# Trunk kernel: the last down weights through the freed up-weight places, the end of the split and tap order, and the last two layer-norm tiles in halves

## The reference, cut to what matters

```python
def conv_glu_ffn(x, w_up, conv_w, conv_b, w_down):
    up = causal_depthwise_conv(x @ w_up, conv_w, conv_b)     # width 3 along the sequence
    gate, val = up[..., :D_FF], up[..., D_FF:]
    return (jax.nn.silu(gate) * val) @ w_down

ffn = conv_glu_ffn(x, ffn_w_up, ffn_conv_w, ffn_conv_b, ffn_w_down)
ple = jax.nn.sigmoid(x @ ple_w_gate) * (p @ ple_w_proj)
x = layer_norm(DEEPNORM_ALPHA * x + ffn + ple, ln2_g, ln2_b)
```

## Time and profile before

| what | before |
| --- | --- |
| median of 3 runs | 1392.42 us (1392.4 to 1392.64) |
| the profiled execution, its own time | 1391.88 us |
| its span | 1389.8 us |
| TensorE busy | 1311.3 us |
| VectorE busy | 860.7 us |
| ScalarE busy | 502.4 us |
| GpSimd busy | 233.2 us |
| mean granted TensorE clock | 0.983 |

### The profile page before, as it was taken

How to read it: one execution, slowest core, us unless ns; L and a number is a source line. 1 busy time by engine, 2 the same in 40 slices (tenths; PEclk the granted TensorE clock), 3 DMA queues, 4 the chain that set the end, 5 groups by cost and what they waited for, 6 DMA issues and landing times.

```text
span 1389.8 us, 16699 instructions
## 1 busy us (share of the span) xinstructions
PE 1311.3 (94%) x6276; PEld 1064.6 (77%) x6276; DVE 860.7 (62%) x1041; ACT 502.4 (36%) x744; POOL 233.2 (17%) x152
## 2 busy tenths in 40 slices
PE   6999999989956999899999999999999999999986
PEld 5787787767855788788888877878787787888785
DVE  3545646544298844633367767677676867677655
ACT  4435545545424322511332423323242323324411
POOL 0000000002182000430001121211111221111125
PEclk9999999989988999999999999999999999999998
DMA  5101101000000311210111201011111101011202
GB/s 224 46 31 31 42 19 45 32 23 24 1 0 32 121 61 62 91 46 31 46 46 46 76 31 60 31 60 45 45 60 59 61 30 60 30 61 46 76 31 106
DMA packets 22948, 71.95 MB, mean 52 GB/s; under 512 B 2544, under 2 KB 2800, under 8 KB 22896
## 3 DMA queue, kind: packets, MB, share of 16 engines
q1 hardware_dynamic: 22896, 71.22, 15.2%
HBM read 67.02 MB, written 4.19 MB: 51 GB/s over the span
## 4 chain that ended last, share of the span: by engine, by line
PE 68%; DVE 12%; ACT 4%; issue 3%; DMA 2%; DVEq 0%; SPq 0%; ACTq 0%
PE ps L677 12%; PE ps L679 12%; PE ps L678 12%; PE ps L1020 7%; PE ps L1018 7%; PE ps L1019 7%; PE ps L771 2%; DMA down_raw<-u_down 2%; DVE conv_ff L1804 1%; ACT conv_ff L1381 1%; PE ps L731 1%; PE ps L755 1%; PE ps L814 1%; DVE w_lo L563 1%; PE ps L1049 1%
## 5 line engine op out<-in xcount | busy, mean ns | idle before, releaser
L677 PE MATMUL ps<-x_hi,w_hi 128*128 128x512 f32 x336 | 141.7, 422 | 14.2 <-DVE x_lo L507 10.6
L678 PE MATMUL ps<-x_lo,w_hi 128*128 128x512 f32 x336 | 134.1, 399 | 0.0
L679 PE MATMUL ps<-x_hi,w_lo 128*128 128x512 f32 x336 | 133.9, 398 | 0.0
L1855 DVE TENSOR_TENSOR acc<-acc,ps 128x512 f32<-128x512 f32 x144 | 96.1, 685 | 53.4 <-PE ps L679 52.9
L1018 PE MATMUL ps<-mix_hi,w_hi 128*128 128x512 f32 x320 | 126.6, 396 | 0.0
L1019 PE MATMUL ps<-mix_lo,w_hi 128*128 128x512 f32 x320 | 126.6, 396 | 0.0
L1020 PE MATMUL ps<-mix_hi,w_lo 128*128 128x512 f32 x320 | 126.6, 396 | 0.0
L677 PE MATMUL ps<-h_hi,w_hi 128*128 128x512 f32 x288 | 114.6, 398 | 1.5 <-DVE acc L1855 1.5
L679 PE MATMUL ps<-h_hi,w_lo 128*128 128x512 f32 x288 | 113.9, 396 | 0.0
L678 PE MATMUL ps<-h_lo,w_hi 128*128 128x512 f32 x288 | 113.9, 395 | 0.0
L2105 POOL TENSOR_TENSOR weight_sums<-raw 128x512 f32<-128x512 f32 x20 | 28.9, 1443 | 493.1 <-DMA raw<-u_up 493.1
(11 more groups left out here) (256 smaller groups left out, 2916.5 us busy)
## 6 DMA issues: line engine op xcount, KB each, us to landing
raw<-u_up SPq DMA_DIRECT2D x44, 512.0 KB, 3.3
raw<-u_in SPq DMA_DIRECT2D x22, 512.0 KB, 3.3
down_raw<-u_down SPq DMA_DIRECT2D x44, 256.0 KB, 2.8
x_stage<-u_x SPq DMA_DIRECT2D x8, 512.0 KB, 8.1
raw<-u_out SPq DMA_DIRECT2D x8, 512.0 KB, 3.2
x_nat<-x_nat SPq DMA_DIRECT2D x8, 512.0 KB, 3.3
raw<-u_gate SPq DMA_DIRECT2D x8, 512.0 KB, 3.3
out<-o_norm SPq DMA_DIRECT2D x8, 512.0 KB, 2.6
```

The lines of the kernel that those rows point to most:

```text
L677: mm(dst, w_hi, x_hi, start=first, stop=False)
L678: mm(dst, w_hi, x_lo, start=False, stop=False)
L679: return mm(dst, w_lo, x_hi, start=False, stop=last)
L1855: v.tensor_tensor(dst, dst, ps[:, DOWN_BANKS[k % 4], :], ALU.add).then_inc(dn_added, 1)
```

## The change

Six edits, all behind the last chunk's up products:

1. D0A/D0B and D1A/D1B of `pp` 1 come as two whole rows of 512 KB into `raw_a` and `raw_b`, each as soon as the last up operand in its place is split. Only D0B/D1B of `pp` 0 still goes through `down_raw`, and it stands ahead of `ln_gain` and `ln_bias` in SyncE's queue.
2. ScalarE and VectorE split the down operands in another order: D0A, D1A of `pp` 0 ahead of h's split, then D0B, D1B of `pp` 1, D0B, D1B of `pp` 0, then D0A and, last, D1A of `pp` 1. `TAIL_SLOT` keeps the places.
3. The taps of the last gate row are split around `combine` step 5, and ScalarE's second `tap` comes ahead of `silu`.
4. In quarter 0, k 2 waits for D0A of `pp` 1 alone, k 3 for D1A.
5. Tile 2q-1 is turned after `jp` 1 instead of `jp` 2, and `affine` follows the statistics at once, ahead of the next `add_last`. `statistics` waits per half.
6. Tiles 6 and 7 are turned in halves: the first half of tile 6 before `jp` 3 of the last quarter, then the first half of 7, the second of 6, the second of 7. Tile 6 is normalized on ScalarE; gain and bias of its first 512 columns are done on GpSimd, of its last 512 on VectorE behind tile 7, which VectorE still does whole. Tile 7 is stored first.

The diff, cut to its core:

```diff
 TAIL_OPS = ([(o, 0) for o in OPERANDS + (A22,)] + [(o, 1) for o in OPERANDS + (A22,)]
-            + [(d, k) for k in range(2) for d in (D0A, D1A, D0B, D1B)])
+            + [(D0A, 0), (D1A, 0), (D0B, 1), (D1B, 1), (D0B, 0), (D1B, 0), (D0A, 1), (D1A, 1)])
+TAIL_SLOT = {(D0A, 0): 0, (D1A, 0): 1, (D0B, 0): 2, (D1B, 0): 3, (D0A, 1): 4, (D1A, 1): 5}
...
+        for i, (o, r) in enumerate(((S4, raw_a), (A22, raw_b))):
+            eng.wait_ge(op_lo_done, lo_count(LASTC, o, 1))
+            eng.dma_start(raw[:, r, :], a["u_down"][2 * LASTC + i]).then_inc(raw_in[r], 16)
+        eng.wait_ge(op_lo_done, lo_count(LASTC, D1A, 0))
+        load_down(LASTC - 1, D0B)
         eng.wait_ge(prod_full, product_count(LASTC, S2, 1))
         eng.dma_start(lng[:, :], a["ln2_g"].partition_broadcast(P)).then_inc(ln_in, 16)
         eng.dma_start(lnb[:, :], a["ln2_b"].partition_broadcast(P)).then_inc(ln_in, 16)
-        eng.wait_ge(op_lo_done, lo_count(LASTC, D1A, 0))
-        load_down(LASTC - 1, D0B)
-        eng.wait_ge(op_lo_done, lo_count(LASTC, D1B, 0))
-        load_down(LASTC, D0A)
-        eng.wait_ge(op_lo_done, lo_count(LASTC, D1A, 1))
-        load_down(LASTC, D0B)
...
+            for h in halves:
+                eng.wait_ge(dn_added, 16 * (LASTC - 1) + 4 * (m // 2) + 2 * h + 2)
+                for kt in range(4 * h, 4 * h + 4):
+                    last = turn(two((1, 3)[m % 2])[:, kt * P:(kt + 1) * P], acc[:, kt, m * P:(m + 1) * P])
+                last.then_inc(o_full, 1)
...
-                if jp in (0, 2):
-                    turn_back(2 * q - 2 + jp // 2)
-        for m in range(MT - 2, MT):
-            turn_back(m)
+                if jp < 2:
+                    turn_back(2 * q - 2 + jp)
+                elif q == 3 and jp == 2:
+                    turn_back(MT - 2, (0,))
+        turn_back(MT - 1, (0,))
+        turn_back(MT - 2, (1,))
+        turn_back(MT - 1, (1,))
...
+        final_statistics(n, (0,))
+        final_statistics(m, (1,))
+        final_statistics(n, (1,))
+        affine(m)
+        eng.wait_ge(stored[n % 4], 16)
+        v.scalar_tensor_tensor(out=y, in0=rows(n), scalar=st[:, n, 12:13], in1=lng[:, :], op0=ALU.subtract,
+                               op1=ALU.mult).then_inc(o_cent, 1)
+        eng.wait_ge(o_sqrt, n + 1)
+        link(v.reciprocal(st[:, n, 13:14], st[:, n, 15:16]))
+        eng.wait_ge(o_cent, 1)
+        v.scalar_tensor_tensor(out=y, in0=y, scalar=st[:, n, 13:14], in1=lnb[:, :], op0=ALU.mult,
+                               op1=ALU.add).then_inc(o_last, 1)
+        eng.wait_ge(o_nrm, m + 1)
+        y = on[:, m % 4, HALF:D]
+        link(v.tensor_tensor(y, y, lng[:, HALF:D], ALU.mult))
+        v.tensor_tensor(y, y, lnb[:, HALF:D], ALU.add).then_inc(o_last, 1)
...
+        m = MT - 2
+        y = on[:, m % 4, 0:HALF]
+        eng.wait_ge(o_nrm, m + 1)
+        link(g.tensor_tensor(y, y, lng[:, 0:HALF], ALU.mult))
+        g.tensor_tensor(y, y, lnb[:, 0:HALF], ALU.add).then_inc(o_bias, 1)
```

More of the change, by code:

```diff
@@ L516, in op_place, with op_raw @@
             return (last_l if lo else last_h)[:, (D0B, D1B).index(o), :]
-        s_ = (position(c, o, pp) + 4) % 6
+        s_ = TAIL_SLOT[(o, pp)] if c == LASTC and o not in PRODUCTS else (position(c, o, pp) + 4) % 6
         return (wl if lo else wh)[:, s_ // 2, s_ % 2 * HALF:(s_ % 2 + 1) * HALF]
-    def op_raw(o):
+    def op_raw(c, o, pp):
+        if c == LASTC and pp and o not in PRODUCTS:
+            return raw[:, raw_a if o in (D0A, D0B) else raw_b, (slice(0, HALF) if o in (D0A, D1A) else slice(HALF, D))]
         return {A11: raw[:, raw_a, 0:HALF], A12: raw[:, raw_a, HALF:D], A22: raw[:, raw_b, HALF:D],
@@ L528, in wait_op_raw @@
         pair = 2 * (c - 1) + pp
-        if o in (A11, A12):
+        if c == LASTC and pp and o not in PRODUCTS:
+            r = raw_a if o in (D0A, D0B) else raw_b
+            eng.wait_ge(raw_in[r], 16 * (loads_before[r] + 2 * LASTC + 1))
+        elif o in (A11, A12):
             eng.wait_ge(raw_in[raw_a], 16 * (loads_before[raw_a] + pair + 1) + 32 * it)
@@ L1106, in chunk, with turn_back @@
             odd(c, it)
-        def turn_back(m):
-            if m % 2 == 0:
-                eng.wait_ge(dn_added, 16 * (LASTC - 1) + 4 * (m // 2 + 1))
+        def turn_back(m, halves=(0, 1)):
             if m == 0:
                 eng.wait_ge(row_done, 4 * CHUNKS)
-            elif m >= 2:
+            elif m >= 2 and 0 in halves:
                 eng.wait_ge(o_nrm, m - 1)
-            for kt in range(KT):
-                last = turn(two((1, 3)[m % 2])[:, kt * P:(kt + 1) * P], acc[:, kt, m * P:(m + 1) * P])
-            last.then_inc(o_full, 1)
+            for h in halves:
[3 more added lines that the diff above has]
+                last.then_inc(o_full, 1)
         for t in range(4):
@@ L1483, in _ @@
         op_hi(c, A22, 1)
-        h_high(c, 0)
         op_hi(c, D0A, 0)
         op_hi(c, D1A, 0)
-        tap(c, 1, 0)
+        h_high(c, 0)
+        op_hi(c, D0B, 1)
+        op_hi(c, D1B, 1)
         op_hi(c, D0B, 0)
         op_hi(c, D1B, 0)
+        tap(c, 1, 0)
+        op_hi(c, D0A, 1)
+        tap(c, 1, 1)
         silu(c, 1)
-        tap(c, 1, 1)
-        op_hi(c, D0A, 1)
         op_hi(c, D1A, 1)
-        op_hi(c, D0B, 1)
-        op_hi(c, D1B, 1)
         h_high(c, 1)
@@ L1961, in _ @@
         op_lo(c, A22, 1)
+        op_lo(c, D0A, 0)
+        op_lo(c, D1A, 0)
         h_low(c, 0)
-        op_lo(c, D0A, 0)
         combine(c, 1, 3)
-        op_lo(c, D1A, 0)
+        op_lo(c, D0B, 1)
+        op_lo(c, D1B, 1)
         combine(c, 1, 4)
-        taps(c, 1, 0)
         op_lo(c, D0B, 0)
         op_lo(c, D1B, 0)
+        taps(c, 1, 0, 0, (1,))
         combine(c, 1, 5)
+        taps(c, 1, 0, 0, (2,))
         op_lo(c, D0A, 1)
-        op_lo(c, D1A, 1)
         taps(c, 1, 1)
         glu(c, 1)
-        op_lo(c, D0B, 1)
-        op_lo(c, D1B, 1)
+        op_lo(c, D1A, 1)
         h_low(c, 1)
```

77 lines of the change are left out of this document (42 added, 35 removed).

## The result

| | before | changed |
| --- | --- | --- |
| median of 6 runs each | 1392.05 us | 1382.63 us (1380.5 to 1386.39) |
| ratio, changed to before | | 0.9937, interval 0.9921 to 0.9953 |
| span of the profiled execution | 1389.8 us | 1380.0 us |
| mean granted clock | 0.983 | 0.985 |

The change makes the kernel faster by 0.5 to 0.8%. The forecast of 1381.1 us was 1.5 us too low and inside the changed kernel's own runs; the range of 1378.0 to 1385.5 holds the median and five of the six runs. The forecast gave no spread for the runs: these six lie over 5.9 us, and eleven of the kernel before, timed beside `a2_changed`, over 5.5. Some of the experiments ask what part one pair of loads has in it.

A forecast was written before the change was run, and what follows sets the result against it. TensorE, busy 1311.3 of 1389.8 us, was taken as the bound, with losses in quarter 0 and a serial VectorE end. Terms -9.4 + 0.4 - 2.3 = -11.3 gave 1381.1 us, range 1378.0 to 1385.5.

The forecast's parts named there:

- The way in: Last 90 us: TensorE loses 11.0 us in quarter 0 to late weight splits and slow clock; VectorE's chain bounds the end.
- Term one: Quarter 0 of `last_down`: quarter 1 starts at 1325.3 instead of 1334.70, -9.4 us.
- the landing L: When the D0B/D1B pair of `pp` 0 lands, before quarter 0: forecast 1310.2, bounds 1309.3 and 1311.3.
- L to h: Serial ScalarE and VectorE work from the pair's landing to h's low part, feeding quarter 0's k 3: 12.2 us.
- The clock: Quarter 0: idle of 1.6 us, less than the 2.45 after which the clock stayed full, so no slow products.
- Term two: Quarters 1 to 3: half a turn of tile 6 newly on TensorE's path in front of `jp` 3, +0.4 us.
- Term three: The end, after the last `add_last`: five operations laid end to end finish at 10.15 instead of 12.4 us, -2.3 us.
- The sum: Whole kernel: -9.4 + 0.4 - 2.3 = -11.3 us, forecast median 1381.1 us.
- The late pair with a cold array: Quarter 0: late pair makes TensorE idle 3.6 us, clock drops, slow products cost 2.1 us; 1385.2 us, chance 0.15.
- The end gives nothing: The end: tile 6's half waits behind GpSimd's earlier tiles or a store, term three is lost; 1383.4 us, chance 0.1.
- they overlap after all: The end: the last VectorE and GpSimd operations run at once; 1379.1 us, chance 0.08.
- The slower case: Before quarter 0: `raw_b`'s row lands at 1320.5 or later and all 11.3 us are lost; past 1392.4 us, chance 0.03.

The follow-up runs named there:

- a2_changed: The changed kernel itself, run once more unaltered against the kernel before; 1382.12 us, ratio 0.9929.
- e3_ln_after: The changed kernel with one wait more: the two layer-norm loads are issued only after the pair for `down_raw` has landed; 1381.42 us, ratio 0.9919.
- e5_old_order: The changed kernel with whole-row loads kept, but splits, taps and TensorE's waits in the order of the kernel before; 1385.32 us, ratio 0.9957.
- e2_tail: The kernel before with only the changed turns, end order and handling of tiles 6 and 7; 1390.63 us, ratio 0.9987.
- e6_no_pool: The changed kernel with tile 6's gain and bias done whole on VectorE, none on GpSimd; 1382.70 us, ratio 0.9930.
- e1_head: The changed kernel with turns, end order and tiles 6 and 7 as in the kernel before; 1387.42 us, ratio 0.9966.
- e8_turns_back: The changed kernel with the odd tiles turned after `jp` 2 again, as in the kernel before; 1382.06 us, ratio 0.9930.
- e4_ln_ahead: The changed kernel with the two layer-norm loads issued ahead of the pair for `down_raw`; 1386.73 us, ratio 0.9956.

## Why the prediction was right, point by point

**The way in.** Two waits of 2.45 and 5.67 and a cold array in quarter 0, and a serial end: both were the places, and behind quarter 0's start nothing else moved by more than 0.5 us.

**Term one, -9.4: measured -8.7** in the profiled execution, -7.6 in a2_changed. What was off is mostly the landing L, the time of one pair of loads. I took 3.08 + 0.9 us from the second issue; it was 4.38 here and up to 6.82 elsewhere. That is 0.4 of the missing 0.7; another 0.2 is that the second of the pair was issued that much later, counted from quarter 0's start. The 0.9 came from one row, `ln_gain` with one load behind it. The pair has a row ahead and two behind, and e3_ln_after shows what it is without the two behind: 3.8. Against that the five traces with them are 0.4 to 3.0 longer. So my 3.98 had the right size for a pair with the row alone beside it, and for another reason than the one that I gave. Everything behind L held: L to h was forecast at 12.2 us and took 12.2 (1311.54 to 1323.73), and did so in every trace where this line bounds. The loads give 6.2 of the 8.7 and the order 2.5, by e5_old_order; I hadn't divided it.

**The clock.** That no product was slow came true, but the reason that I gave, an idle time shorter than the 2.45 that had left the clock full, is not enough. In e2_tail a wait of 2.31 us was followed by twelve products, and the clock fell while TensorE was still at them; the section on the hardware has the rows. In the traces with the changed kernel's order no clock fell where one wait stood alone, up to 3.01 us; e2_tail's 2.31 had one of 0.24 ahead of it. So the 2.45 was no safe mark, and that the forecast of no slow products held is in part luck.

**Term two, +0.4: measured +0.5.** The turned half tile in front of `jp` 3, in every run alike.

**Term three, -2.3: measured -2.3.** The five operations end at the last add + 9.98 (forecast 10.15). That they exclude each other stood on one row of 3.27 us; e6_no_pool took one side away, and the lengths came back to what they are alone. The section of the Trainium skill that I named (SBUF — State Buffer, "Who interferes with whom") is borne out: 2.10, 1.68 and 2.12 us together, 1.28, 0.6 and 1.2 alone (the 0.6 and the 1.2 are half of the 1.22 and 2.4 that 1024 columns take).

**The sum.** -8.7 + 0.5 - 2.3 = -10.5, and 0.75 us from the start of the program, in another place of each execution, make the 9.8 by which the spans differ.

**The rivals.** The late pair with a cold array had 0.15. Its lateness is no case apart but the upper end of what this kernel's pair does (a2_changed), and e1_head shows it with the cold array. Its price of 2.1 us for the cold array was read as 36 slow products; in the trace of the kernel before about 20 of the 36 were slow, the rest full, which gives about the same sum. e1_head's 15 products at 1.2 GHz cost 1.6. I should have put L's upper bound where four loads share the engines, not at the longest load that had run alone. "The end gives nothing" and "they overlap after all" are refuted by an end of 13.2 us in the seven traces that treat tiles 6 and 7 as the change does (they wanted 15.5 and 11.2 us), and by e6_no_pool. The slower case needed `raw_b`'s row to be over ten us late; the rows into `raw` landed in 3.1 to 3.5 us in every trace.

## What to carry to other kernels

A load on the critical chain can be slowed by loads issued behind it as well as ahead: hold back what has time (here one wait on the pair's semaphore). Here that took 0.4 to 3.0 us off one landing in the traces, and too little off the medians to be told from their noise. Before sharing elementwise work between VectorE and GpSimd, look for one row that is too long while the other engine runs: if two-operand SBUF work excludes itself, give it all to the faster engine. When a wait on a whole-width operation is left, ask how much of it the next product needs.

## What the runs showed of the hardware that was not expected

The length of TensorE's idle time alone doesn't tell whether its clock falls. It stayed at 2.4 GHz after 2.82 (e8_turns_back), 3.01 (a2_changed) and 3.29 us (e5_old_order), and fell to 1.2 GHz after 3.00 (e1_head) and 3.02 us (e4_ln_ahead), for 15 slow products each. In the two that fell there had been another wait of 0.98 us some 6 us before, and in e4_ln_ahead one of 0.76 before that; but e5_old_order had two, of 0.24 and 0.68.

Nor does the fall have to lie in the idle time. In e1_head and e4_ln_ahead it came 0.6 us after TensorE had started again, behind four products at full clock. In the kernel before it came at 1326.0, some 3.5 us into the wait of 5.67. In e2_tail it came 1.4 us after a wait of 2.31 had ended, at the end of twelve products and before the wait of 5.16 began. Two stretches of its windows (columns as in the earlier trace rows):

```profile
1324.40:1325.00 0.60, 0.60 (x8) 0.60 (x7) 0.56 (x2) 0.00 (x0) 0.00 (x0) 1.00 0.53 130
...
1325.20:1325.40 0.20, 0.20 (x2) 0.00 (x0) 0.20 (x1) 0.00 (x0) 0.00 (x0) 0.50 0.78 205
```

What decides stays open. e1_head's slow products cost some 1.6 us (24 products in 4.48 us, where 24 at 0.12 are 2.9).
